# Placing the matmul operands of a transformer kernel modulo 256 bytes, and the MLP's wide product made narrow

## The reference

```
for l in (0, 1):
    x = x + mixer(rmsnorm(x))        # w_in 1024 -> 6080: three attentions (8, 4 and 8 heads) and their gates,
                                     # three branch products 512 -> 1024, summed by sigmoid gates, w_out
    x = x + (gelu(g) * a) @ w_down   # a, g = depthwise conv of 3 taps over rmsnorm(x) @ w_up, 1024 -> 2 * 2816
x = final rmsnorm(x)
rwkv7 time mix and a causal attention, post-norm with ALPHA; MLP 0
dilated attention, post-norm; MLP 1
MLP: x = layernorm(ALPHA * x + square(max(h @ w1, 0)) @ w2)     # 1024 -> 4096 -> 1024
```

## Time and profile before

| | |
|---|---|
| median of 3 runs | 1602.79 us (1602.32 to 1603.22) |
| the profiled execution's own time | 1601.72 us |
| its span, first to last instruction | 1599.8 us |
| TensorE busy | 1571.2 us, 11814 matmuls |
| TensorE weight loads | 1421.1 us, 11814 |
| VectorE busy | 1093.3 us |
| ScalarE busy | 947.5 us |
| GpSimd busy | 295.2 us |
| DMA | 272.77 MB, mean 170 GB/s |

### The profile page before, as it was taken

How to read it: one execution, slowest core, us unless ns; L and a number is a source line. 1 busy time by engine, 2 the same in 40 slices (tenths; PEclk the granted TensorE clock), 3 DMA queues, 4 the chain that set the end, 5 groups by cost and what they waited for, 6 DMA issues and landing times. The chain is left out here.

```text
span 1599.8 us, 28596 instructions
## 1 busy us (share of the span) xinstructions
PE 1571.2 (98%) x11814; PEld 1421.1 (89%) x11814; DVE 1093.3 (68%) x1702; ACT 947.5 (59%) x1563; POOL 295.2 (18%) x214
## 2 busy tenths in 40 slices
PE   9999999999999999999999999989999999999998
PEld 7999998999899999989998897768888899878886
DVE  5775656887457665568864677678944678789744
ACT  6777756665457877566654665346533666665531
POOL 0000210443000002104420143016500021118300
PEclk9999999999999999999999999999999999999999
DMA  8343454565553434545555531225565435345651
GB/s 330 120 154 137 150 194 183 193 231 183 189 185 105 172 119 149 215 152 200 195 186 183 225 117 71 75 95 203 208 217 204 189 132 185 106 184 186 237 197 65
DMA packets 42321, 272.77 MB, mean 170 GB/s; under 512 B 4816, under 2 KB 4944, under 8 KB 13392
## 3 DMA queue, kind: packets, MB, share of 16 engines
q1 hardware_dynamic: 41184, 265.18, 46.7%
q10 hardware_dynamic: 1008, 5.77, 1.0%
HBM read 269.88 MB, written 1.05 MB: 169 GB/s over the span
## 5 line engine op out<-in xcount | busy, mean ns | idle before, releaser
L317 DVE TENSOR_TENSOR b_wlo<-b_wraw,b_whi 128x2048 fp32r<-128x2048 f32 (+3 forms) x261 | 565.2, 2169 | 180.2 <-PE b_ps L471 124.9
L309 ACT ACTIVATE b_whi<-b_wraw 128x2048 fp32r<-128x2048 f32 (+3 forms) x262 | 466.3, 1781 | 200.1 <-PE b_ps L471 148.3
L390 PE MATMUL b_ps<-b_H,b_whi 128*128 128x256 f32 x1704 | 483.2, 284 | 0.2
L393 PE MATMUL b_ps<-b_H,b_wlo 128*128 128x256 f32 x1704 | 476.3, 280 | 0.0
L392 PE MATMUL b_ps<-b_H,b_whi 128*128 128x256 f32 x1704 | 476.2, 279 | 0.0
L390 PEld LDWEIGHTS b_ps<-b_H,b_whi 128*128 128x128 f32 x1704 | 321.0, 188 | 8.3 <-issue 6.8
L392 PEld LDWEIGHTS b_ps<-b_H,b_whi 128*128 128x128 f32 x1704 | 321.1, 188 | 0.6
L393 PEld LDWEIGHTS b_ps<-b_H,b_wlo 128*128 128x128 f32 x1704 | 320.9, 188 | 0.0
L436 PE MATMUL b_ps<-b_H,b_whi 128*128 128x512 f32 x448 | 155.7, 391 | 0.0
L1597 POOL TENSOR_TENSOR b_fl<-b_ab,b_fh 128x256 fp32r<-128x256 f32 x44 | 93.6, 2128 | 213.4 <-ACT b_fh L1570 213.4
L437 PE MATMUL b_ps<-b_H,b_wlo 128*128 128x256 f32 x448 | 126.3, 282 | 0.0
(11 more groups left out here) (367 smaller groups left out, 2721.9 us busy)
## 6 DMA issues: line engine op xcount, KB each, us to landing
b_wraw<-in_w SPq DMA_DIRECT2D x221, 1024.0 KB, 4.8
b_wraw<-in_w SPq DMA_DIRECT2D x35, 512.0 KB, 3.6
b_wraw<-in_w SPq DMA_DIRECT2D x6, 768.0 KB, 6.0
b_bias<-in_rpb SPq DMA_DIRECT2D x8, 512.0 KB, 6.5
b_gains<-in_gains ACTq DMA_DIRECT2D x4, 1024.0 KB, 4.9
b_X<-in_x ACTq DMA_DIRECT2D x2, 512.0 KB, 5.4
b_cA<-in_cA SPq DMA_DIRECT2D x2, 512.0 KB, 6.1
out<-b_X SPq DMA_DIRECT2D x4, 256.0 KB, 2.1
```

The source lines that it names most:

```text
L309: e.activation(whi[u % NHI][:, 0:n], raw[u % NRAW][:, 0:n], ACT.Copy).then_inc(up("w_hi", "whi", u))
L317: e.tensor_tensor(wlo[u % NLO][:, 0:n], raw[u % NRAW][:, 0:n], hi.bitcast(F32), ALU.subtract).then_inc(up("w_lo", "wlo", u))
L390: e.matmul(out, wh, x.hi[:, kk, :], start=k == 0, stop=False)
L393: ins = e.matmul(out, wl, x.hi[:, kk, :], start=False, stop=last)
```

## The change

- `place(ctx, past)` inserts a gap so that the next tensor starts at `past` modulo 256 bytes from the weights.
- H2 is moved ahead of X and c1 and placed at -64 (it was at +32). What follows H2 at the top level now ends at -64.
- In the Mixer y0 (was at 0), cqn and ckn (were at -32), y1 and y2 (were at -32) are all placed at -64.
- In Ffn, Mlp, Rwkv and Dilated fh, gh, ym and ydh are placed at 0, where they were before; the gap only makes up for the new end of the top level.
- `wide_pe` goes. Tiles 4 to 31 of the MLP's first product use `tile_pe`, so three matmuls of 256 moving columns for each k block in the place of one of 512 and one of 256. ScalarE's copy to `low` goes, with the buffers and its waits, and VectorE's addition becomes the plain copy.

```diff
+LINE = 256
+MOVED = -64
+LOADED = 0
+    def next_free():
+        return -(-nc.sbuf_base // 32) * 32
+
+    def place(ctx, past):
+        n = (at_line + past - next_free()) % LINE
+        if n:
+            sb(ctx, "gap", [P, n // 4])
+    at_line = next_free()
     raw = ring(top, "wraw", NRAW, [P, UNIT])
     whi = ring(top, "whi", NHI, [P, UNIT], F32R)
     wlo = ring(top, "wlo", NLO, [P, UNIT], F32R)
+    place(top, MOVED)
+    H2 = sb(top, "H", [P, 8, 2, T], F32R)
     X = sb(top, "X", [P, 2, D])
     c1 = sb(top, "c1", [P, sum(w for _, w in at1.values())])
-    H2 = sb(top, "H", [P, 8, 2, T], F32R)
...
+                place(s1, MOVED)
                 self.y0 = sb(s1, "y0", [P, 8, T], F32R)
...
+                place(s1, MOVED)
                 cqn = [sb(s1, "cqn", [P, 3, T], F32R) for _ in range(2)]
...
+                    place(s2, MOVED)
                     self.y1, self.y2 = sb(s2, "y1", [P, 8, T], F32R), sb(s2, "y2", [P, 8, T], F32R)
...
+                place(s1, LOADED)
                 fh, fl = sb(s1, "gh", [P, 32, T], F32R), sb(s1, "gl", [P, 32, T], F32R)
-                self.r, self.low = ring(s1, "relu", 4, [P, T]), ring(s1, "low", 4, [P, T])
+                self.r = ring(s1, "relu", 4, [P, T])
...
-                    wide_pe(e, w, self.w1, j)
+                    tile_pe(e, w, self.w1, j)
...
-                    if j >= 4:
-                        if p >= 4:
-                            w.wait_ge(*at("low_free", self.l, p - 4))
-                        w.wait_ge(*at("full", (self.w1.key, j)))
-                        e.activation(self.low[p % 4][:, :], banks.tile((self.w1.key, j))[:, T:2 * T], ACT.Copy).then_inc(up("low", "low", self.l, j))
...
-                if j < 4:
-                    e.tensor_copy(R, out).then_inc(banks.free((self.w1.key, j)))
-                else:
-                    w.wait_ge(*at("low", self.l, j))
-                    e.tensor_tensor(R, self.low[p % 4][:, :], out, ALU.add).then_inc(banks.free((self.w1.key, j)))
-                sig.same(("low_free", self.l, p), ("free", (self.w1.key, j)))
+                e.tensor_copy(R, out).then_inc(banks.free((self.w1.key, j)))
...
```

More of the change, by code:

```diff
@@ L423, in tile_pe @@
                 sig.same(("unit", u), ("full", (job.key, j)))
[L427 to L440, removed]
     def row_blocks(job):
```

## The result

The changed kernel takes 1581.65 us (median of 6 executions, 1581.05 to 1585.99) against 1602.55 us of the kernel before: a ratio of 0.9877, 95% interval 0.9863 to 0.9892. That is 1.2% faster; the forecast was 1582 us.

What follows compares the result with a forecast made beforehand. TensorE's start-to-start distances were taken to bound the kernel; savings of 13.4 + 3.3 + 1.0 + 2.9 = 20.6 us took the profiled 1601.7 to 1581.1, plus 1.1 for the median: 1582 us, range 1562 to 1606.

Steps and rivals of the forecast that it cites:

- What bounds the kernel: Whole kernel: TensorE, busy 1571.2 of 1599.8 us, sets the time through the distance between starts of consecutive matmuls.
- Duration less 163: Unbroken rows of matmuls: the distance between starts is a matmul's duration less 163 ns.
- H at -64: Narrow matmuls with H moving: distance falls from 116.7 to 113.5 ns, saving 13.4 us on 4176 of 5112.
- y and latents: Narrow matmuls with y or latents moving, placed at -64: from 118 to 113.5 ns, saving 3.3 us on 732.
- H and merged y loaded from -64: Row form loading H or y: 230 ns, from 232 on H, saving 1.0 us on H and nothing on y.
- The MLP: MLP's 448 wide-form k blocks become 1344 narrow matmuls: 155.4 us falls to 152.5 at 113.5 ns, saving 2.9 us.
- rival 4: MLP: VectorE takes over as the limit and gives back 2.9 us, 1585 us; no separate chance given.
- The sum: Whole kernel: 13.4 + 3.3 + 1.0 + 2.9 = 20.6 us saved, for a forecast of 1582 us.
- Rival 1: Narrow matmuls: the place helps less, distance about 116 ns, kernel at 1599 us; chance 0.12.
- Rival 2: All matmuls: the place does nothing, narrow stays at 116.7 ns, MLP costs 1.4 us more, 1604 us; chance 0.10.
- Rival 3: Matmuls at -64: a bad place, narrow goes to 120 ns, 23.6 us lost, 1626 us; chance 0.21.

Runs made afterwards that it cites:

- the nine places of the table: Runs with H, y and latents at -96, -80, -64, -48, 0, +64, +96 or 128, or H alone at +32; 1581.65 to 1619.74 us.
- the places alone: All placements and H2's move as in the change, but the MLP keeps its wide form, against the kernel before: 1587.76 us, ratio 0.9923.

## Why the prediction was right, point by point

**What bounds the kernel** held. TensorE's starts are what time is made of: distances fell in the narrow form and the kernel with them. Over the nine places of the table the kernel's time rises with the distance of its long stretches, from 1581.65 us at 113 ns to 1619.74 at 120 (the two places at 119.2 and 119.3 ns are 0.3 us apart, less than can be told).

**Duration less 163** held at the new distances too: 276 is 113, 281 is 118.

**H at -64.** Forecast was one distance of 113.5, for 13.4 us. The better level is 113.3, the estimate nearly met it; but the step took it for granted that a place has one distance. In the first trace the mean over H is 114.8. Counted from the starts, the matmuls on H took 609.5 us before and 597.5 with the places alone: 12.0 us. It came out near the forecast because two errors offset, which is luck: a third of the matmuls at 117.8, against Rwkv and half of Dilated which I had written off. From its first to its last narrow start Rwkv gained 1.9 us, 0.6 of it in the unbroken 192 matmuls at its start, and Dilated 1.2. So the stretches for which 13.4 us were forecast gave about 9.

**y and latents.** Forecast 3.3 us, measured 2.1: y fell from 69.9 to 67.8 us, and the latents gained nothing; in all traces at -64 they run at 117.8, near the 118.3 they had at -32. That is a mis-sized term: the latents are at the poorer level in each of the five traces at -64.

**H and merged y loaded from -64.** Forecast 230 against a measured 229.4 on H; before, the starts give 233.2 and not the 232 that the step read from durations. The matmuls of 512 columns on H take 1.2 us less with their waits, for the forecast 1.0, and those on y 0.6 us less, for nothing. That the level place is the best for a loaded activation is confirmed: 228.0 over all and 227 mostly on H at 0.

**The MLP.** Forecast 2.9 us at 113.5, and this is the other mis-sized term. In the profiled execution one MLP lost (73.2 us from first to last group against 71.8) and one won (70.4): nothing in the sum, 155.5 us before and after. And the step compared with the wide form at its old place only, while at -64 it costs 3 us more; this doesn't touch the sum, but the worth of the edit. VectorE was 55.5 of 63 us busy in the first MLP and 58.0 of 62 in the second, and TensorE never waited for it: rival 4 did not come.

**The sum** in the profiled execution: 12.5 (H, 12.0 with the places alone) + 2.1 (y) + 1.8 (row form) + 0 (MLP) = 16.4 us in matmul distances. The shorter row matmuls on H gave 0.4 more and the other matmuls took 1.1 back; its own time fell by 15.7, to 1585.99. The forecast of 20.6 is met by the medians (20.9), as the profiled execution is the slowest of the six. I have no trace of the quick ones; the first MLP's stretch at 113.3 would account for 2.8 of the 4.9 us between them, and that is argued, not shown.

**The rivals.** Rival 1 (116) is wrong for H, 113.4. Rival 2 falls with the runs at nine places. By the Trainium skill ("TensorE: Matmul & The Clock Gate", Part 2, step-by-step) loading weights doesn't steal read bandwidth from the running matmul, yet the kernel's time moves from 1581.65 to 1619.74 us by places alone. Whether it is the bandwidth of the reads that is shared isn't shown. Rival 3 was real elsewhere: at 0, +64, +96, 128, -48, -80 and -96 the kernel is slower than before, by up to 1.2%. So seven of the nine places are slower: the odds for a place picked without a measurement were worse than the 0.21 I gave it, which shows how much of the forecast hung on one extrapolated step.

## What to carry to other kernels

Where TensorE's starts follow each other without a gap and the distance is above columns divided by clock, compare equal shapes with operands at different places, and then measure the places modulo 256 bytes; don't extrapolate from one to the next, as 16 bytes can cost 6 ns of 113. A choice between two forms of a product is to be measured again after the places have changed. And read the minimum and the median of each stretch before believing a mean: a mixture of two levels looks like a small gain.

## What the runs showed that I had not expected

- A stretch of narrow matmuls at -64 keeps one of two distances, 113.3 or 117.8 ns, over up to 910 matmuls, with equal instructions and addresses; a row of other work ahead of it can change which, and so can a repetition of the same program. In long stretches the other places with two are -96 (117.3, 118.7) and 128 (118.7, 120.0); in short ones also +32, +64 and -48.
- The wide form and the narrow form disagree on the place: 512 moving columns of H take 228 ns at +32 and 235 at -64, 256 take 116.7 and 113.3.
- The row form is best with both operands level (226.8 ns on g, 228.0 on H), the narrow form is at its worst there (120.0 ns, as at +96).
